# High and low token halves side by side in nine phases of a fused two-block kernel on one Trainium2 core

## The reference, cut to what matters

```python
def swiglu(x, w_gu, w_down):
    g, u = jnp.split(x @ w_gu, 2, axis=-1)
    return (jax.nn.silu(g) * u) @ w_down
...
        x = x + 0.5 * swiglu(rmsnorm(x, ffn1_norm[l]), ffn1_w_gu[l], ffn1_w_down[l])
        h = rmsnorm(x, mix_norm[l])
        z = h @ w_in[l]
        u = jax.nn.gelu(z[..., COL_U:COL_V], approximate=False)
        v = jax.nn.gelu(z[..., COL_V:COL_CQ], approximate=False)
...
        x = x + merged @ w_out[l]
        x = x + 0.5 * swiglu(rmsnorm(x, ffn2_norm[l]), ffn2_w_gu[l], ffn2_w_down[l])
```

## Time and profile before

| what | value |
|---|---|
| median of 3 runs | 1729.25 us (1725.32 to 1734.23) |
| the profiled execution, span from first to last instruction | 1725.9 us |
| PE busy | 1632.4 us (95% of the span) |
| PE weight loads busy | 1545.4 us (90%) |
| DVE busy | 1086.8 us (63%) |
| ACT busy | 837.4 us (49%) |
| POOL busy | 411.2 us (24%) |
| mean granted TensorE clock | 0.977 of full speed |

### The profile page before, as it was taken

The page is one execution under the profiler, slowest core; times in us unless marked ns, Lnnn a source line. Parts: engine busy times, 40 slices in busy tenths (PEclk is TensorE's granted clock), DMA queues, the critical chain, the costliest instruction groups (busy, mean ns, idle before and its releaser), DMA issues.

```text
span 1725.9 us, 32053 instructions
## 1 busy us (share of the span) xinstructions
PE 1632.4 (95%) x12871; PEld 1545.4 (90%) x12871; DVE 1086.8 (63%) x1528; ACT 837.4 (49%) x1225; POOL 411.2 (24%) x387
## 2 busy tenths in 40 slices
PE   6998988889999999999999999999999999889998
PEld 6896878769989999897899999999988688889998
DVE  6783554536468884656688847665553865666653
ACT  7772444454455554554655545444443155554432
POOL 0001454410115652001255524321100000212210
PEclk9995999999999999999999999999999999999999
DMA  7441111015434445452255465544633533445543
GB/s 267 157 150 53 52 52 45 8 39 193 154 131 171 172 147 182 157 209 77 98 175 191 142 205 191 194 172 162 224 134 116 212 122 117 153 152 193 193 165 125
DMA packets 42414, 252.49 MB, mean 146 GB/s; under 512 B 5504, under 2 KB 7664, under 8 KB 20304
## 3 DMA queue, kind: packets, MB, share of 16 engines
q1 hardware_dynamic: 38416, 233.20, 38.3%
q0 software_dynamic: 3904, 17.98, 3.3%
HBM read 249.99 MB, written 1.17 MB: 146 GB/s over the span
## 4 chain that ended last, share of the span: by engine, by line
PE 73%; DVE 9%; issue 8%; ACT 6%; DMA 3%; POOL 0%; ACTq 0%; DVEq 0%; POOLq 0%; SPq 0%
PE bank L422 19%; PE bank L424 19%; PE bank L423 19%; DVE w_lo L297 3%; ACT w_hi L294 2%; PE bank L1237 2%; PE bank L1245 2%; DMA work<-rows_scratch 1%; DVE work L818 1%; PE bank L1252 1%; DVE rs L577 1%; PE bank L624 1%; ACT work L2275 1%; DMA sq<-rows_scratch_q 1%; DVE mix L583 1%
## 5 line engine op out<-in xcount | busy, mean ns | idle before, releaser
L422 PE MATMUL bank<-work_r,w_hi 128*128 128x256 f32 (+2 forms) x3248 | 925.3, 285 | 23.8 <-DVE w_lo L297 14.3
L423 PE MATMUL bank<-work_r,w_hi 128*128 128x256 f32 (+2 forms) x3248 | 918.5, 283 | 0.0
L424 PE MATMUL bank<-work_r,w_lo 128*128 128x256 f32 (+2 forms) x3248 | 918.2, 283 | 0.0
L297 DVE TENSOR_TENSOR w_lo<-ring,w_hi 128x2048 fp32r<-128x2048 f32 (+2 forms) x233 | 497.0, 2134 | 325.1 <-ACT w_hi L294 325.1
L422 PEld LDWEIGHTS bank<-work_r,w_hi 128*128 128x128 f32 x3248 | 617.4, 190 | 35.0 <-DVE w_lo L297 19.8
L294 ACT ACTIVATE w_hi<-ring 128x2048 fp32r<-128x2048 f32 (+2 forms) x233 | 408.3, 1754 | 450.7 <-PE bank L424 450.3
L423 PEld LDWEIGHTS bank<-work_r,w_hi 128*128 128x128 f32 x3248 | 616.3, 190 | 0.3
L424 PEld LDWEIGHTS bank<-work_r,w_lo 128*128 128x128 f32 x3248 | 616.2, 190 | 0.0
L1455 POOL TENSOR_TENSOR work<-work 128x272 f32<-128x272 f32 (+1 forms) x44 | 92.0, 2090 | 137.2 <-ACT work L1417 137.2
L533 POOL TENSOR_TENSOR sq<-sq 128x256 f32<-128x256 f32 (+2 forms) x36 | 57.5, 1598 | 251.0 <-ACT sq L511 250.2
L1443 DVE SCALAR_TENSOR_TENSOR work<-work,params_sb 128x272 f32<-128x272 f32 (+1 forms) x176 | 99.1, 604 | 5.1 <-DVE work L1443 0.2
(11 more groups left out here) (431 smaller groups left out, 1935.2 us busy)
## 6 DMA issues: line engine op xcount, KB each, us to landing
ring<-in_stream SPq DMA_DIRECT2D x166, 1024.0 KB, 4.8
ring<-in_stream SPq DMA_DIRECT2D x64, 704.0 KB, 4.1
ring<-in_stream SPq DMA_DIRECT2D x10, 768.0 KB, 4.3
work<-rows_scratch POOLq DMA_DIRECT2D x4, 1632.0 KB, 7.5
work<-rows_scratch POOLq DMA_DIRECT2D x4, 544.0 KB, 8.8
work<-rows_scratch_o POOLq DMA_DIRECT2D x1, 2176.0 KB, 10.0
ring<-in_stream SPq DMA_DIRECT2D x3, 512.0 KB, 7.5
work<-rows_scratch_m POOLq DMA_DIRECT2D x1, 1088.0 KB, 7.0
```

Source lines behind the costliest of these rows:

```text
L297: eng.tensor_tensor(w_lo[:, slot, 0:size], raw_w, w_hi[:, slot, 0:size].bitcast(F32), ALU.subtract).then_inc(lo_done, 1)
L422: pe.matmul(out, w_hi[:, slot, at:at + P], hi, start=first, stop=False)
L423: pe.matmul(out, w_hi[:, slot, at:at + P], lo, start=False, stop=False)
L424: mm = pe.matmul(out, w_lo[:, slot, at:at + P], hi, start=False, stop=last)
```

## The change

In nine phases (the table `WIDE`) the high and the low tokens of a block lie side by side in 512 columns. The two products with high weights become one product of 512 columns that fills a whole bank, so that the bank holds two halves: columns 0 to 255 with high x high and low x high, columns 256 to 511 with high x low. The product with low weights still takes the 256 high columns. The halves are added when the bank is emptied: in up2 and up3 ACT copies the low half to memory and DVE adds the other half and then multiplies by the scale; in the in phases DVE does copy, add and multiply; in the down phases and mix_out DVE adds to `hs` twice. In those chains each operation waits for the one before on its own engine. The buffers of the tokens move so that the halves lie side by side. In in_gates and branches nothing is changed but, in in_gates, the address of the tokens.

```diff
+WIDE = ("up2", "down2", "in_uv", "in_cq_kr", "in_ckv", "in_qm", "mix_out", "up3", "down3")
...
-                        if ph.split:
+                        if name in WIDE:
+                            both = x(m, kx)
+                            pe.matmul(ps[b % BANKS], w_hi[:, slot, at:at + P], both, start=first, stop=False)
+                            mm = pe.matmul(out, w_lo[:, slot, at:at + P], both[:, 0:n], start=False, stop=last)
+                        elif ph.split:
...
+        X2 = area(A2_AT, DB, 2 * SEQ, of=work_r)
+        A2_HI, A2_LO = X2[:, :, 0:SEQ], X2[:, :, SEQ:2 * SEQ]
...
+        def summed_up_dve(dve, un, turn, m, dst):
+
+            if m == 0:
+                S.begin("up_sum")
+            dve.wait_ge(*S.at("lo_half", m, turn=turn))
+            S.inc(dve.tensor_tensor(dst, dst, un.bank(m)[:, 0:SEQ], ALU.add), "up_sum")
+            S.own(dve, "up_sum", turn)
+            un.free(dve.tensor_tensor(dst, dst, scale2, ALU.mult), m)
+
         def up_act(act, name):
+            turn = lambda un: un.u + (FB if name == "up3" else 0)
+
             def body(un):
+                S.begin("lo_half")
+                act.wait_ge(*S.at("hid_pool", turn=turn(un)))
+                for m in range(2):
+                    un.ready(act, m)
+                    dst = h2_new[:, un.j % 4, :] if m else sg2[un.j % 4]
+                    S.inc(act.activation(dst, un.bank(m)[:, SEQ:2 * SEQ], ACT.Copy), "lo_half", m)
+
+            def late(un):
                 un.was_read(act, 0)
                 S.begin("up_silu")
                 S.inc(act.activation(sg2[un.j % 4], sg2[un.j % 4], ACT.Silu), "up_silu")
-            each_product(act, name, 2, body, ACT.Silu, split="hi", lag=1)
+            each_product(act, name, 2, body, ACT.Silu, split="hi", late=late, lag=1, split_last=True)
...
             def body(un):
                 un.ready(dve, 0)
-                un.free(dve.tensor_tensor(sg2[un.j % 4], un.bank(0)[:, 0:SEQ], scale2, ALU.mult), 0)
+                summed_up_dve(dve, un, turn(un), 0, sg2[un.j % 4])
                 un.ready(dve, 1)
-                dve.wait_ge(*S.at("hid_pool", turn=turn(un)))
-                un.free(dve.tensor_tensor(h2_new[:, un.j % 4, :], un.bank(1)[:, 0:SEQ], scale2, ALU.mult), 1)
+                summed_up_dve(dve, un, turn(un), 1, h2_new[:, un.j % 4, :])
...
+        def add_halves(dve, un, m, dst):
+
+            S.begin("halves")
...
+            S.inc(dve.tensor_copy(dst, un.bank(m)[:, SEQ:2 * SEQ]), "halves")
+            S.own(dve, "halves", turn)
+            S.inc(dve.tensor_tensor(dst, dst, un.bank(m)[:, 0:SEQ], ALU.add), "halves")
+            S.own(dve, "halves", turn)
+
+        def summed_dve(dve, un, m, dst):
+
+            add_halves(dve, un, m, dst)
+            un.free(dve.tensor_tensor(dst, dst, scale2, ALU.mult), m)
+
+        def residual_dve(dve, un, scale):
+
+            dst = h2[:, un.u, :]
+            S.begin("added")
...
+            S.inc(dve.scalar_tensor_tensor(out=dst, in0=un.bank()[:, SEQ:2 * SEQ], scalar=scale, in1=dst, op0=ALU.mult, op1=ALU.add), "added")
+            S.own(dve, "added", turn)
+            un.free(dve.scalar_tensor_tensor(out=dst, in0=un.bank()[:, 0:SEQ], scalar=scale, in1=dst, op0=ALU.mult, op1=ALU.add))
+
         def down_dve(dve, name, late=None):
             each_product(dve, name, 1, lambda un: (
-                un.ready(dve), un.free(dve.scalar_tensor_tensor(out=h2[:, un.u, :], in0=un.bank()[:, 0:SEQ], scalar=0.5,
-                                                                in1=h2[:, un.u, :], op0=ALU.mult, op1=ALU.add))),
+                un.ready(dve), residual_dve(dve, un, 0.5)),
...
-                un.ready(dve), un.free(dve.tensor_tensor(dst(un.j), un.bank()[:, 0:SEQ], scale2, ALU.mult))), turns=0, split="lo")
+                un.ready(dve), summed_dve(dve, un, 0, dst(un.j))), turns=0, split="lo")
...
-                un.ready(dve), un.free(dve.tensor_tensor(h2[:, un.u, :], un.bank()[:, 0:SEQ], h2[:, un.u, :], ALU.add))),
+                un.ready(dve), residual_dve(dve, un, 1.0)),
```

More of the change, by code:

```diff
@@ L113, with kind_of @@
 PLAN, SLABS, STREAM_WORDS = plan()
+HALVES_OF = {}
+def kind_of(name):
+    return "residual" if name in ("down2", "mix_out", "down3") else "up" if name in ("up2", "up3") else "input"
+for _name in WIDE:
+    HALVES_OF[_name] = sum(PLAN[_n].products for _n in HALVES_OF if kind_of(_n) == kind_of(_name))
 SLAB_OF = [ph for ph in PLAN.values() for _ in range(ph.slabs)]
@@ L436, in stream_pe @@
                             pe.wait_ge(bank_free[b % BANKS], b // BANKS + 1)
-                        hi, lo = x(0, k)
                         slot, at = (SPLIT_AT[ph.slab0] + p // ph.parts) % SPLIT_SLOTS, (p % ph.parts * kb + k) * P
                         out = ps[b % BANKS][:, 0:n]
-                        pe.matmul(out, w_hi[:, slot, at:at + P], hi, start=(k == 0), stop=False)
-                        pe.matmul(out, w_hi[:, slot, at:at + P], lo, start=False, stop=False)
-                        mm = pe.matmul(out, w_lo[:, slot, at:at + P], hi, start=False, stop=(k == kb - 1))
+                        if name in WIDE:
+                            both = x(0, k)
+                            pe.matmul(ps[b % BANKS], w_hi[:, slot, at:at + P], both, start=(k == 0), stop=False)
+                            mm = pe.matmul(out, w_lo[:, slot, at:at + P], both[:, 0:n], start=False, stop=(k == kb - 1))
+                        else:
+                            hi, lo = x(0, k)
+                            pe.matmul(out, w_hi[:, slot, at:at + P], hi, start=(k == 0), stop=False)
+                            pe.matmul(out, w_hi[:, slot, at:at + P], lo, start=False, stop=False)
+                            mm = pe.matmul(out, w_lo[:, slot, at:at + P], hi, start=False, stop=(k == kb - 1))
                         if k == kb - 1:
@@ L491, in x, with wide_input @@
                 return hi[:, k, 0:n], lo[:, k, 0:n]
+            return x
+        def wide_input(both, arrive):
+            seen = set()
+            def x(m, k):
+                if k not in seen:
+                    seen.add(k)
+                    arrive(k)
+                return both[:, k, :]
             return x
@@ L1753, in program @@
         keep_at = 6144
-        hid2_hi, hid2_lo = (area(keep_at + i * FB * SEQ, FB, SEQ, of=work_r) for i in range(2))
+        hid2 = area(keep_at, FB, 2 * SEQ, of=work_r)
+        hid2_hi, hid2_lo = hid2[:, :, 0:SEQ], hid2[:, :, SEQ:2 * SEQ]
         sg2 = [area(keep_at + 2 * FB * SEQ + i * SEQ, SEQ) for i in range(4)]
@@ L2684, in _ @@
             mem_norm_pe(pe)
-            stream_pe(pe, "down2", hidden_input(pe, hid2_hi, hid2_lo, SEQ, "hid_pool", 4), SEQ)
+            stream_pe(pe, "down2", wide_input(hid2, hidden_arrives(pe, "hid_pool", 4)), SEQ)
             in_x = a2_parts(8)
@@ L2721, in _ @@
             mem_v_pe(pe, 3)
[L2722 removed]
+            gates_pe(pe, lambda m, k: (A2_HI[:, k, :], A2_LO[:, k, :]))
             def branch_input(m, k):
@@ L2728, in _ @@
             stream_pe(pe, "branches", branch_input, SEQ)
-            stream_pe(pe, "mix_out", split_input(pe, M_HI, M_LO, SEQ, by_step(pe, 9)), SEQ)
+            stream_pe(pe, "mix_out", wide_input(M2, by_step(pe, 9)), SEQ)
             stream_pe(pe, "up3", a2_parts(10), SEQ, lead=1, after_lead=lambda: norm_pooled_pe(pe, 5, "pre", 5, SEQ))
-            stream_pe(pe, "down3", hidden_input(pe, hid2_hi, hid2_lo, SEQ, "hid_pool", FB + 4), SEQ)
+            stream_pe(pe, "down3", wide_input(hid2, hidden_arrives(pe, "hid_pool", FB + 4)), SEQ)
     return S.seen
```

15 lines of the change are left out of this document (9 added, 6 removed).

## The result

The changed kernel takes 1754.99 us (median of 4 runs, 1751.53 to 1759.53), the kernel before in the same comparison 1727.28 us (1723.11 to 1734.23): the medians are 27.7 us apart. The ratio of the two, run against run, is 1.014, with a 95% interval of 1.0101 to 1.0179: the changed kernel is slower by 1.4%, some 24 us, where I had forecast 1735.1 us and a range that ended at 1744. The profiled execution spans 1749.8 us against the 1725.9 before.

What follows compares the result with a forecast made beforehand. Two clocks were taken to bound it: PE's stream and the PE-ACT-DVE slab loop. Losses in the in phases (+7.4 - 0.5) and mix_out (+3.2) outweighed gains elsewhere: +5.85 on 1729.25, 1735.1 us, range 1727 to 1744.

Steps and rivals of the forecast that it cites:

- the price of the wide product: PE stream, nine phases: a 512-column product takes 216 ns, so a triple falls from 340 to 329.4 ns.
- the loop in up: up2, up3: PE finishes slab s, ACT rounds s+2, DVE subtracts, PE starts s+2; 5.06 us undisturbed, against PE's 5.27.
- my dearest end: PE stream: if the surcharge grows with the columns, the wide product takes 227 ns and nothing is saved.
- My loop of 5.38 on the mean: up2, up3: slabs of 5.27 and 5.49 us in turn, 5.38 each, gaining 0.06 per slab of a possible 0.17.
- w_hi's delay: up2, up3: the second bank's copy and the Silu stand ahead of ACT's w_hi, which comes 0.58 us later.
- The alternation: up2, up3: DVE's low part meets POOL in one slab (5.49 us), runs ahead of it in the next (5.06 again).
- the rival of POOL in the way: up2, up3: POOL's second operation always blocks the low part for 0.74 us; +5.7, 1740.8 us; chance 0.21.
- my 5.80: up2, up3: slab loop with POOL blocking, 5.06 + 0.74 us; a pair of slabs was taken as 11.07.
- the last residual: End of the kernel: it waits for one more residual operation on DVE, +0.45 us.
- The cycle: in_uv: two evacuations each gain two DVE operations (0.92 us), so the cycle takes 7.1 us against PE's 5.27.
- my 7.4: in phases: the longer evacuation chains make in_ckv start 7.4 us later, all on the path.
- Saves nothing: PE stream: rival that the wide product saves next to nothing, 1740.5 us, or nothing at all, 1742; chance 0.13.

Runs made afterwards that it cites:

- e1: Changed kernel with each 512-column product split into two 256-column products, one into each half of the bank, new evacuations kept: 1750.66 us, ratio 1.0108.
- e2: Changed kernel with its wide products but the evacuations of the kernel before, leaving high x low out of the result: 1738.48 us, ratio 1.0040.
- e8: Changed kernel with the change in up2, down2, up3 and down3 only, not in the in phases and mix_out: 1742.45 us, ratio 1.0091.
- e12: Kernel before with the change in in_uv, in_cq_kr, in_ckv and in_qm only: 1741.12 us, ratio 1.0054.
- e7: Changed kernel with high and low tokens in separate arrays, the wide product reading two rows of 256: 1752.30 us, ratio 1.0146.
- e9: Kernel before with the three short products of each block reordered so that no two neighbours share weights: 1735.91 us, one run.

## Why the prediction was wrong

Two steps failed: the price of the wide product, and the loop in up. **The price of the wide product** is the first. I took 216 ns, from the plain float32 product of 256 columns, on the ground that the 6.7 ns over the columns come from the weight load and are paid once. It takes 235. Even my dearest end, 227 ns with nothing saved, was too low, because it doubled the fast 113.4, and the wide stream is never at that rate. Instead of 10.7 ns saved per block, 13 are lost wherever the short ones ran fast. The Trainium skill, page "TensorE: Matmul & The Clock Gate", section "Wait — 56ns, not 53.3ns?", whose rule gave 215.8 ns for 512 columns, is off here by as much as my row; the measurement decides.

The trace of before could have warned me in two places. The 118.0 ns of down2, which I called a sign that 113.4 is no law, was the second rate, and I still built on the first. And its products of 272 columns, which I didn't read, contradict a fixed surcharge. In up0 their window is

```profile
540.00:600.00 60.00, 60.00 (x489) 60.00 (x488) 53.23 (x72) 34.15 (x42) 36.55 (x31) 1.00 0.50 180
```

486 starts there are 123.3 ns apart: for 16 columns more it is 10 ns over 113.4, where 2.4 GHz gives 6.7. In another part of the first block the products have 258 columns:

```profile
824.00:840.00 16.00, 16.00 (x136) 16.00 (x135) 6.88 (x3) 9.53 (x16) 8.83 (x5) 1.00 0.36 132
```

134 starts are 120.0 ns apart, so two columns more already cost 6.6 ns over 113.4: the time doesn't grow evenly with the columns, and 113.4 at 256 columns is the exception. At 123.3 / 272 = 0.453 ns per column 512 columns take 232, at 120.0 / 258 = 0.465 they take 238 (both estimates). That two points of the same kind speak against a fixed surcharge, and one point of another kind (plain float32) for it, should have put the range's end well over 227.

**up2 and up3** were forecast as -1.1 each and came out as +4.9 and +5.1. My loop of 5.38 on the mean failed twice over: PE's slab is 5.65 instead of 5.27, and the loop, seen on a fast stream, is 5.55 to 5.65 instead of 5.06 and 5.49 in turn (e1). This second miss alone would have brought the sum to 1741 to 1745 us (0.17 to 0.27 over 5.38, 36 slabs; an estimate). Of the loop's pieces w_hi's delay was right (0.77 for 0.78). The alternation was wrong: the low part meets POOL at each slab and takes 2.75 to 2.80, as in the rival of POOL in the way, with 0.46 to 0.51 lost to it instead of my 0.74; and PE starts 0.13 behind it where I had 0.04. I had priced that rival too low: if POOL is in the way of every slab, every slab takes the longer loop, and my 5.80 would have made 0.42 more on each of the 36, some 15 us, not the 5.7 of a slab in two. The Trainium skill, page "SBUF — State Buffer", section "SBUF: two separate sides", lets the loser of the port pair wait for the whole instruction; here it lost two thirds of one that had started 0.09 ahead. A price for the new evacuations in up would have been 5.55 to 5.65 against 5.44, some 4 to 7.5 us over 36 slabs; in the changed kernel it is hidden under a stream that is just as slow.

**down2** came out at +2.3 for -0.6: no gain from the stream, and the second residual in the loop, since e2, without the new evacuations, is at 0.0, and e8, with them in down2 but not in the in phases, at +2.0. **down3 and the end** came out at +2.4 for -1.4: 176 blocks at 13.3 ns are 2.3, and the last residual was as forecast, two operations 0.46 apart (it answers to the earlier trace rows):

```profile
1743.97 0.42 DVE L1945 SCALAR_TENSOR_TENSOR hs<-bank,hs 128x256 f32<-128x256 f32 x1 [3.88 <-PE bank L435]
1744.43 0.42 DVE L1947 SCALAR_TENSOR_TENSOR hs<-bank,hs 128x256 f32<-128x256 f32 x1
```

**in phases and mix_out** were right in mechanism and size. The cycle was forecast at 7.1 and is 7.08, with the three dependent operations 0.45 and 0.46 apart:

```profile
1256.92 0.42 DVE L1930 COPY work<-bank 128x256 f32<-128x256 f32 x1
1257.37 0.42 DVE L1932 TENSOR_TENSOR work<-work,bank 128x256 f32<-128x256 f32 x1
1257.83 0.42 DVE L1938 TENSOR_TENSOR work<-work,rs 128x256 f32<-128x256 f32 x1
```

That made +6.6 for 6.9 by the bounds of the table; by e12 the chain up to in_ckv is 7.3 us for my 7.4. mix_out's cycle was forecast at 6.97 (6.05 and two residuals) and is 6.97; +4.0 for 3.2. Leaving these five phases out gives back 9.9 us (e7 against e8), 10.1 by the forecast.

**The rivals.** "Saves nothing" was the nearest: it had the mechanism on PE, and its 1742 fell short by the price above and by the loop in up. **The baseline** was a trap of its own: I scaled from one execution that had drawn the fast rate in up2, up3 and down3. The medians hold some slow ones, and in the in phases and mix_out part of the stream lies in waits, so against them the wide stream alone costs 8.4 us (e2), not the 17 us that 1264 blocks at 13.3 ns would give.

## What to carry to other kernels

Before merging two products into a wider one, take the start-to-start time of the same type at two widths, and in more than one phase; a surcharge over the columns can grow with them, and then the merge only removes instructions. When a stream and the loop beside it are both near the bound, price each by itself: here either one brought the slab to 5.65 us or close to it, and undoing one would not have brought the time back. A single profile can hold a lucky draw, so look at whether stretches with the same instructions run at the same rate before counting savings of a few ns each.

## What was not expected of the hardware

- A float32r product of 256 columns starts either 113.3 or 117.8 ns after the one before, at a granted clock of 1.00 in both cases. The rate is set at a pause of PE, holds up to the next one (294 of 295 stretches) and differs between executions of the same program. Of 402 stretches 301 were fast. A restart that comes again with the same timing brings the same rate again (e1, up3).
- One of 512 columns takes 235 ns beside short ones (80 of 80 stretches) and 233.3 among its like (8 of 8). One of 272 takes 123.3 in most stretches, one of 258 takes 120.0, 6.7 more than the fast rate of 256. One of 128 takes 111.7, hardly less than one of 256.
- Plain float32 products with 16 columns of tokens start 27 ns apart with 16 columns of weights each and 213 with 128, at a granted clock of 0.50: there the weight load sets the pace.
- Whether two neighbouring products share their weights, and whether low and high tokens lie in one piece, made no difference to the rates (e9, e7). What makes the wide product dear, and what decides the draw of the short one, stays open.
